# Chunk outputs and states of the second recurrence issued inside the next chunk's levels, with GpSimd held behind the block copies

## The chip, the cores and the metric

The kernel runs on one core of one Trainium2 chip. The metric is the device time of one execution in microseconds (us), the median of the runs. The engines are TensorE (PE, with its weight loads as PEld), VectorE (DVE), ScalarE (ACT), GpSimd (POOL) and SyncE (SP), which issues the loads. A time such as 1374.25 is us from the start of the profiled span.

## The reference, cut to what matters

The program is two transformer-like blocks over 512 tokens of width 1024. The first has two layers, and each layer has a mixer with two recurrences; the change is in the second one (HGRN2), which runs forward and backward over the sequence with four heads of 128:

```
def _hgrn2_scan(q, k, i, logf):
    # S_t = diag(f_t) S_{t-1} + k_t i_t^T,  o_t = S_t^T q_t
    def step(state, inp):
        q_n, k_n, i_n, b_n = inp          # b_n: running sum of logf in the chunk
        dec = jnp.exp(jnp.where(incl, b_n[:, :, :, None, :] - b_n[:, :, None, :, :], -jnp.inf))
        att = jnp.einsum('bhtd,bhsd,bhtsd->bhts', q_n, k_n, dec)
        o = (jnp.einsum('bhtd,bhdv->bhtv', q_n * jnp.exp(b_n), state)
             + jnp.einsum('bhts,bhsv->bhtv', att, i_n))
        last = b_n[:, :, -1:, :]
        state = (state * jnp.exp(last[:, :, 0, :])[..., None]
                 + jnp.einsum('bhsd,bhsv->bhdv', k_n * jnp.exp(last - b_n), i_n))
        return state, o
```

## The kernel before, in words

`hgrn_stage` does this once for each layer, so twice in an execution, with chunks of 128 tokens: four chunks `m` = 0 to 3. There are two lanes, `d` = 0 (forward) and 1 (backward), which go side by side. Every engine has its own instruction stream, written out by hand, and semaphores `S[...]` tie them; nothing reorders the streams.

The attention matrix `AT` of a chunk is built in seven levels, n = 0 to 6, of growing distance between query and key. For level n DVE makes scaled queries and keys (`scaled`, L1812 and L1813: two 128x256 products for a lane, both inputs in SBUF), and PE multiplies them (`level`, L1646 and L1649, `last_level`, L1660) into one of two accumulator banks of the lane. Levels 0 to 4 are merged by DVE into `AC` (`gather`, L1821), level 5 and level 6 are copied from PSUM into `AT` by ACT (`assembled`, L1763 and L1767), and the diagonal blocks `AC` are copied into `AT` by DVE (`blocks_placed`, L1832: four copies of 32x128 for a lane). The factors come from exponents: PE sums log decays (`exponents`, L1618 and L1619) into banks 0 to 3, and ACT exponentiates them (`decays`, L1753). `prepare` (L1596, L1604 and L1605) turns the next chunk's keys and sums, inside the levels of the chunk before it.

From `AT` PE makes the chunk's outputs (`outputs`, L139, with the part from the old state for m > 0) and its new state (`state`, L1679). Before, for chunks 0 and 1 these stand between one chunk's last level and the next chunk's first product (`diagonal`, L1629), and write the accumulator banks. Only chunk 2 has them inside the levels of chunk 3, in banks 0 to 3 (`late`). ACT copies the outputs out (L1800), DVE adds the new state to the decayed one (`grow_state`, L1854 for the first, L1852 afterwards), and ACT decays that for the next chunk (`state_decayed`, L1780).

GpSimd has four products of 128x512 at each of the chunk boundaries 0/1 and 1/2 and two at 2/3, both inputs in SBUF: `keys_decayed` (L1570) and `queries_decayed` (L1576). Before, the first of them waits for the last scaled product of the chunk, so it starts together with DVE's block copies.

Of the kernel before, what the change touches and what calls it, by code (L numbers as in the profile page):

```python
# [1506 lines left out]
def hgrn_stage(nc, signals, PS, C, CR, LF, KK, HI, HQ, X, O, new, early):  # L1507
# [21 lines left out]
    with signals.stage(*[f"hgrn_{n}{d}" for n in kinds for d in lanes]) as sems:  # L1529
# [5 lines left out]
        late = lambda m: m == CH - 2  # L1535
# [18 lines left out]
        with nc.Block() as block:  # L1554
# [8 lines left out]
            def _(pool):  # L1563
                def keys_decayed(m, d):
                    pool.wait_ge(S["es"][d], m + 1)
                    if m:
                        pool.wait_ge(S["x"][1], 2 * m * LEVELS)
                    if m == 2:
                        pool.wait_ge(S["st"][d], 1)
                    pool.tensor_tensor(kd_of(m, d), keys(m, d).rearrange("p (h n) -> p h n", h=4), B[d]["ES"][:, :, :], ALU.mult).then_inc(S["kd"][d], 1)  # L1570
# [20 lines left out]
            def _(pe):  # L1591
                def turned_keys(m, d):
                    if m:
                        pe.wait_ge(S["e"][1], 8 * m)
                    for h in H4:
                        last = pe.transpose(hx(d, h), keys(m, d)[:, h * P:(h + 1) * P], C[:, IDENT, :])  # L1596
                    last.then_inc(S["kt"][d], 1)

                def suffix(m, d):
                    pe.wait_ge(S["fl"][d], m + 1)  # L1600
                    if m:
                        pe.wait_ge(S["e"][1], 8 * m)
                    b = B[d]
                    pe.matmul(PS[:, 2 + d, :], CR[:, d, 8, :], b["FH"][:, :], start=True, stop=False)  # L1604
                    pe.matmul(PS[:, 2 + d, :], CR[:, d, 8, :], b["FL"][:, :], start=False, stop=True).then_inc(S["suf"][d], 1)  # L1605
# [15 lines left out]
                def diagonal(m, d):  # L1621
                    pe.wait_ge(S["ktc"][d], m + 1)
                    if m == CH - 1:
                        pe.wait_ge(S["af"][d], m)
                    elif m:
                        pe.wait_ge(S["oc"][d], m)
# [5 lines left out]
                def level(m, d, n):  # L1632
                    pe.wait_ge(S["x"][d], 2 * (m * LEVELS + n + 1))
                    if n >= 2:
                        pe.wait_ge(S["ac"][d], m * SMALL_LEVELS + n - 1)
                    elif n == 1:
                        pe.wait_ge(S["diac"][d], m + 1)
                    elif m == CH - 1:
                        pe.wait_ge(S["af"][d], m)
                    elif m:  # L1640
                        pe.wait_ge(S["su"][d], m)
# [50 lines left out]
                for m in range(CH):  # L1692
                    for d in lanes:
                        diagonal(m, d)
                    for n in range(LEVELS):
# [7 lines left out]
                        if m == CH - 1 and n in (1, 3):  # L1703
                            for e in lanes:
                                pe.wait_ge(S["e"][e], 8 * CH)
                            d = n // 2
                            outputs(CH - 2, d)
                            state(CH - 2, d)
# [9 lines left out]
                    for d in lanes:  # L1718
                        if not late(m):
                            outputs(m, d)  # L1720
                        if m < CH - 2:
                            state(m, d)

            @block.scalar
            def _(act):
# [29 lines left out]
                def assembled(m):  # L1755
                    for d in lanes:
                        act.wait_ge(S["a"][d], m * LEVELS + LEVELS - 1)
                        if m:
                            act.wait_ge(S["o"][d], m)
                        else:  # L1760
                            act.wait_ge(S["mk"][0], 5)
                        for one, two in zip(early_quarters[d], late_quarters[d]):
                            act.copy(B[d]["AT"][one, :, two], small(d, LEVELS - 2)[one])  # L1763
                    for d in lanes:
                        one, two = FIRST[d], SECOND[d]
                        act.wait_ge(S["a"][d], (m + 1) * LEVELS)
# [15 lines left out]

                for m in range(CH):
                    if 0 < m < CH - 1:
                        for d in lanes:
                            state_decayed(m, d)
                    decays(m, 1, 1)
                    if m + 1 < CH:
                        for d in lanes:
                            high(m + 1, d)  # L1790
                        prepared(m + 1)
# [5 lines left out]
                    if m < 2:  # L1797
                        for d in lanes:
                            act.wait_ge(S["o"][d], m + 1)
                            act.copy(of_chunk(chunk(m, d)), per_head(acc(d, 1))).then_inc(S["oc"][d], 1)  # L1800

            @block.vector
            def _(dve):
# [24 lines left out]
                def blocks_placed(m, d):  # L1828
                    dve.wait_ge(S["ac"][d], (m + 1) * SMALL_LEVELS)
                    dve.wait_ge(S["o"][d], m) if m else dve.wait_ge(S["mk"][0], 5)  # L1830
                    for rows in QUARTERS:
                        last = dve.tensor_copy(B[d]["AT"][rows, :, rows], B[d]["AC"][rows, :, :])  # L1832
# [28 lines left out]
                for m in range(CH):  # L1861
# [4 lines left out]
                    for n in range(LEVELS):  # L1866
                        if 0 < n < LEVELS - 1:
                            for d in lanes:
                                scaled(m, d, n + 1)
                        if n < SMALL_LEVELS:  # L1870
# [5 lines left out]
                        if m == CH - 1 and n in (2, 4):  # L1876
                            d = n // 2 - 1
                            add_output(CH - 2, d)
                            grow_state(CH - 2, d)
                    for d in lanes:  # L1880
                        blocks_placed(m, d)
                    if m + 1 < CH:
                        for n in range(2):
                            for d in lanes:
                                scaled(m + 1, d, n)
                    for d in lanes:
                        if m < CH - 2:
                            grow_state(m, d)
                        if m == CH - 1:
                            add_output(m, d)  # L1890
# [1527 lines left out]
```

## Time and profile before

| | us |
|---|---|
| runs, median of 3 | 2850.24 (2844.2 to 2854.49) |
| the profiled execution, its own time | 2841.33 |
| its span in the trace | 2839.5 |
| PE busy | 2726.6 (96% of the span) |
| DVE busy | 1513.2 (53%) |
| ACT busy | 1199.3 (42%) |
| POOL busy | 850.1 (30%) |

The two executions of the stage lie at 362.9 to 458.9 and at 1350.0 to 1443.3 of the span. The shares of the page are means over stages that have different limits; what the change is worth is decided in these two stretches, some 7% of the span.

### The profile page before, as it was taken

Reading aid. Unit: us, or ns where it says so; the run is one execution under the profiler, and the core shown is the slowest. Engines: PE = TensorE matmul, PEld = TensorE weight load, DVE = VectorE, ACT = ScalarE, POOL = GpSimd, SP = SyncE. Lnnn points to the kernel's source line nnn. Section 1 sums busy time; section 2 is a strip of 40 time slices with the busy share of each in tenths; the row PEclk is TensorE's granted clock in tenths of the full one; section 3 lists DMA queues with packets and bytes.
Section 4 is the critical chain, followed back from the end, with each engine's and each line's share of the span. In section 5 each row is a group of like instructions: output and inputs, shape, how many; then the busy total and the mean of one; then the engine's idle time right before and its main releaser. Section 6 shows DMA issues by size and latency. Waiting matters only on the chain. (4 is left out here: it accounts for less than half of the span.)

```text
span 2839.5 us, 48429 instructions
## 1 busy us (share of the span) xinstructions
PE 2726.6 (96%) x20434; PEld 2226.6 (78%) x20434; DVE 1513.2 (53%) x2273; ACT 1199.3 (42%) x1941; POOL 850.1 (30%) x476
## 2 busy tenths in 40 slices
PE   8989988999999999899989999999999999999999
PEld 6777877888888877778778888888787778888887
DVE  7565577357526475655863565364886543521120
ACT  5564665233212245645742332222545543442331
POOL 2343020024444423520200344443002224344433
PEclk9989999999999999899999999999999999999999
DMA  5102103333323331021033333232522223333322
GB/s 177 58 4 88 60 3 98 100 115 96 104 82 104 89 98 53 4 89 60 3 113 96 111 97 110 83 108 71 123 76 75 65 65 98 97 97 97 97 82 82
DMA packets 414585, 236.30 MB, mean 83 GB/s; under 512 B 24244, under 2 KB 404770, under 8 KB 413730
## 3 DMA queue, kind: packets, MB, share of 16 engines
q1 hardware_dynamic: 413490, 233.18, 28.2%
q8 instruction: 163, 2.67, 0.4%
q14 instruction: 52, 0.43, 0.1%
q10 hardware_dynamic: 880, 0.02, 0.0%
HBM read 226.88 MB, written 6.29 MB: 82 GB/s over the span
## 5 line engine op out<-in xcount | busy, mean ns | idle before, releaser
L2425 POOL TENSOR_TENSOR WLO<-RAW,WHI 128x1024 fp32r<-128x1024 f32 (+1 forms) x199 | 522.1, 2629 | 964.5 <-ACT WHI L2261 964.5
L146 PE MATMUL PS<-HHI,WHI 128*128 128x512 f32 x2016 | 795.8, 395 | 5.4 <-DVE WLO L3157 2.2
L147 PE MATMUL PS<-HLO,WHI 128*128 128x512 f32 x2016 | 787.2, 390 | 0.0
L148 PE MATMUL PS<-HHI,WLO 128*128 128x512 f32 x2016 | 786.7, 390 | 0.0
L146 PEld LDWEIGHTS PS<-HHI,WHI 128*128 128x128 f32 x2016 | 379.9, 188 | 98.1 <-issue 7.4
L147 PEld LDWEIGHTS PS<-HLO,WHI 128*128 128x128 f32 x2016 | 380.2, 189 | 80.3 <-issue 2.6
L148 PEld LDWEIGHTS PS<-HHI,WLO 128*128 128x128 f32 x2016 | 380.1, 189 | 79.8
L2261 ACT CAST WHI<-RAW 128x1024 fp32r<-128x1024 f32 (+1 forms) x202 | 221.7, 1102 | 508.4 <-PE PS L148 492.8
L2414 DVE TENSOR_TENSOR X<-X,PS 128x512 f32<-128x512 f32 x48 | 33.0, 688 | 334.1 <-PE PS L148 334.1
L3219 POOL TENSOR_TENSOR WLO<-RAW,WHI 128x1280 fp32r<-128x1280 f32 x31 | 91.3, 2947 | 317.7 <-ACT WHI L3102 317.7
L2397 DVE SCALAR_TENSOR_TENSOR ACC<-GP,PARS,ACC 128x512 f32<-128x512 f32 x88 | 163.0, 1853 | 3.1
L146 PE MATMUL PS<-MHI,WHI 128*128 128x512 f32 x384 | 150.4, 392 | 7.4 <-DVE LHID L2355 4.2
L148 PE MATMUL PS<-MHI,WLO 128*128 128x512 f32 x384 | 149.6, 390 | 0.0
L147 PE MATMUL PS<-MLO,WHI 128*128 128x512 f32 x384 | 149.5, 389 | 0.0
L202 ACT CAST WHI<-RAW 128x1536 fp32r<-128x1536 f32 (+1 forms) x50 | 81.6, 1632 | 99.1 <-PE PS L148 87.8
L2390 DVE TENSOR_TENSOR GP<-PS,RS 128x512 f32<-128x512 f32 x44 | 30.4, 692 | 152.5 <-PE PS L148 127.7
L206 DVE TENSOR_TENSOR WLO<-RAW,WHI 128x1536 fp32r<-128x1536 f32 (+1 forms) x50 | 97.3, 1946 | 22.8 <-ACT WHI L202 21.6
L2303 ACT ACTIVATE ACC<-ACC 128x512 f32<-128x512 f32 x44 | 27.9, 634 | 176.5 <-DVE ACC L2397 176.5
L146 PE MATMUL PS<-YHI,WHI 128*128 128x512 f32 x256 | 100.5, 393 | 1.5 <-DVE WLO L2359 1.2
L146 PE MATMUL PS<-WHI,HHI 128*128 128x512 f32 (+1 forms) x256 | 96.1, 375 | 5.1 <-DVE WLO L1456 5.1
L148 PE MATMUL PS<-YHI,WLO 128*128 128x512 f32 x256 | 99.7, 390 | 0.0
L147 PE MATMUL PS<-YLO,WHI 128*128 128x512 f32 x256 | 99.7, 389 | 0.0
(502 smaller groups left out, 4757.2 us busy)
## 6 DMA issues: line engine op xcount, KB each, us to landing
RAW<-in_w_up SPq DMA_DIRECT2D x88, 512.0 KB, 3.7
RAW<-in_w_mlp SPq DMA_DIRECT2D x64, 512.0 KB, 4.0
RAW<-in_w_in SPq DMA_DIRECT2D x46, 512.0 KB, 3.8
RAW<-in_w_down SPq DMA_DIRECT2D x32, 704.0 KB, 4.4
RAW<-in_w_in SPq DMA_DIRECT2D x20, 1024.0 KB, 5.0
RAW<-in_w_gate SPq DMA_DIRECT2D x32, 512.0 KB, 4.0
RAWQ<-in_w_in SPq DMA_DIRECT2D x24, 512.0 KB, 3.7
RAW<-in_w_out SPq DMA_DIRECT2D x24, 512.0 KB, 5.2
```

Source lines behind the costliest of these rows:

```text
L146: e.matmul(out, wh, xh, start=first and n == 0, stop=False)
L147: e.matmul(out, wh, xl, start=False, stop=False)
L148: last = e.matmul(out, wl, xh, start=False, stop=final and n == len(quads) - 1)
L202: self.hi_st.done(act.copy(self.hi[:, s], self.raw[:, s]), f"unit{s}")
L206: self.lo_st.done(dve.tensor_tensor(self.lo[:, s], self.raw[:, s], self.hi[:, s], ALU.subtract), f"unit{s}")
L2261: ac.done(act.copy(slot(WHI, u), source(u)), f"hi{u}")
L2303: ac.done(act.activation(acc, acc, ACT.Silu), f"silu{i}")
L2390: dv.done(dve.tensor_tensor(gp[:, 1:513], tile_bank((i, 0)), RS[:, :], ALU.mult), f"g{i}")
L2397: dv.done(dve.scalar_tensor_tensor(acc, gp[:, n:n + 512], tap(n), acc, ALU.mult, ALU.add), f"tap{n}_{i}")
L2414: dv.done(dve.tensor_tensor(X[:, m, :], X[:, m, :], PS[:, 6 + m % 2, :], ALU.add), f"x{g}_{m}")
L2425: pool.tensor_tensor(slot(WLO, u), source(u), slot(WHI, u), ALU.subtract).then_inc(lo_s, 1)
L3219: pool.tensor_tensor(WLO[:, u % 3], RAW[:, u % 3], WHI[:, u % 3], ALU.subtract).then_inc(lo_s, 1)
```

## The change

`late` now holds for chunks 0, 1 and 2. So the outputs and the state of chunk m-1 are issued in chunk m behind level 1 (lane 0) and level 2 (lane 1), and write banks 0 to 3, which the exponents use at other times. DVE's `grow_state` goes to the same levels (ahead of the gather of level 2 and of level 3), and ACT's copy of the outputs and `state_decayed` stand behind `decays(m, 1, 1)` and the casts of `high`. The copy of level 5 into `AT` (four 32x128 copies from PSUM for the two lanes of a chunk) goes from ACT to DVE (`level_placed`) behind the block copies, and the semaphore `as` is given only behind it. GpSimd's keys of chunk m wait for `as` of both lanes. The scaled products of levels 0 and 1 of the next chunk go lane by lane.

```
-        late = lambda m: m == CH - 2
+        late = lambda m: m < CH - 1
...
                 def keys_decayed(m, d):
                     pool.wait_ge(S["es"][d], m + 1)
                     if m:
-                        pool.wait_ge(S["x"][1], 2 * m * LEVELS)
+                        for e in lanes:
+                            pool.wait_ge(S["as"][e], m)
...
                 def turned_keys(m, d):
...
+                    if m > 1:
+                        pe.wait_ge(S["oc"][d], m - 1)
...
                 def suffix(m, d):
...
+                    if m > 1:
+                        pe.wait_ge(S["su"][d], m - 1)
...
                 def diagonal(m, d):
                     pe.wait_ge(S["ktc"][d], m + 1)
-                    if m == CH - 1:
-                        pe.wait_ge(S["af"][d], m)
-                    elif m:
-                        pe.wait_ge(S["oc"][d], m)
+                    if m:
+                        pe.wait_ge(S["as"][d], m)
...
-                        if m == CH - 1 and n in (1, 3):
+                        if m and n in (1, 2):
                             for e in lanes:
-                                pe.wait_ge(S["e"][e], 8 * CH)
-                            d = n // 2
-                            outputs(CH - 2, d)
-                            state(CH - 2, d)
+                                pe.wait_ge(S["e"][e], 8 * m + 8)
+                            outputs(m - 1, n - 1)
+                            state(m - 1, n - 1)
...
-                    for d in lanes:
-                        if not late(m):
-                            outputs(m, d)
-                        if m < CH - 2:
-                            state(m, d)
+                for d in lanes:
+                    outputs(CH - 1, d)
...
                 for m in range(CH):
-                    if 0 < m < CH - 1:
-                        for d in lanes:
-                            state_decayed(m, d)
                     decays(m, 1, 1)
                     if m + 1 < CH:
                         for d in lanes:
                             high(m + 1, d)
+                    if 0 < m < CH - 1:
+                        for d in lanes:
+                            output_kept(m - 1, d)
+                            state_decayed(m, d)
+                    if m + 1 < CH:
                         prepared(m + 1)
...
                     for rows in QUARTERS:
-                        last = dve.tensor_copy(B[d]["AT"][rows, :, rows], B[d]["AC"][rows, :, :])
+                        dve.tensor_copy(B[d]["AT"][rows, :, rows], B[d]["AC"][rows, :, :])
+
+                def level_placed(m, d):
+                    dve.wait_ge(S["a"][d], m * LEVELS + LEVELS - 1)
+                    for one, two in zip(early_quarters[d], late_quarters[d]):
+                        last = dve.tensor_copy(B[d]["AT"][one, :, two], small(d, LEVELS - 2)[one])
                     last.then_inc(S["as"][d], 1)
...
+                        if m and n in (2, 3):
+                            grow_state(m - 1, n - 2)
...
-                        if m == CH - 1 and n in (2, 4):
-                            d = n // 2 - 1
-                            add_output(CH - 2, d)
-                            grow_state(CH - 2, d)
+                        if m == CH - 1 and n in (2, 3):
+                            add_output(CH - 2, n - 2)
                     for d in lanes:
                         blocks_placed(m, d)
+                    for d in lanes:
+                        level_placed(m, d)
                     if m + 1 < CH:
-                        for n in range(2):
-                            for d in lanes:
+                        for d in lanes:
+                            for n in range(2):
                                 scaled(m + 1, d, n)
-                    for d in lanes:
-                        if m < CH - 2:
-                            grow_state(m, d)
```

Two places show how the streams move. The first is DVE at the boundary of chunks 0 and 1, in the first layer. Before (L1832 are the block copies, L1812 and L1813 the scaled products, L1854 `grow_state`, L1865 the masked diagonal):

```order
L1832 COPY hAT_1<-hAC_1 32x4x32 x8
L1812 TENSOR_TENSOR hX_1<-HQ,X 128x256
L1813 TENSOR_TENSOR hX_1<-hKT_1,X 128x256
L1812 TENSOR_TENSOR hX_1<-HQ,hE_1 128x256
L1813 TENSOR_TENSOR hX_1<-hKT_1,hE_1 128x256
L1812 TENSOR_TENSOR hX_1<-HQ,X 128x128x2
L1813 TENSOR_TENSOR hX_1<-hKT_1,X 128x128x2
L1812 TENSOR_TENSOR hX_1<-HQ,hE_1 128x128x2
L1813 TENSOR_TENSOR hX_1<-hKT_1,hE_1 128x128x2
L1854 COPY hST_1<-PS 128x512 x2
L1865 TENSOR_TENSOR hAC_1<-PS,hEYE 128x128 x2
```

And in the changed kernel, where lines have other numbers:

```order
L1824 COPY hAT_1<-hAC_1 32x4x32 x8
L1829 COPY hAT_1<-PS 32x4x32 x4
L1804 TENSOR_TENSOR hX_1<-HQ,X 128x256
L1805 TENSOR_TENSOR hX_1<-hKT_1,X 128x256
L1804 TENSOR_TENSOR hX_1<-HQ,X 128x128x2
L1805 TENSOR_TENSOR hX_1<-hKT_1,X 128x128x2
L1804 TENSOR_TENSOR hX_1<-HQ,hE_1 128x256
L1805 TENSOR_TENSOR hX_1<-hKT_1,hE_1 128x256
L1804 TENSOR_TENSOR hX_1<-HQ,hE_1 128x128x2
L1805 TENSOR_TENSOR hX_1<-hKT_1,hE_1 128x128x2
L1862 TENSOR_TENSOR hAC_1<-PS,hEYE 128x128 x2
```

Four PSUM copies have come in (L1829), lane 1's products stand behind both of lane 0's, and `grow_state` has left for the levels of chunk 1.

The second is PE behind the last exponents of the same boundary. Before (L139 the outputs, L1679 the states, L1629 the diagonal, L1646 levels):

```order
L139 MATMUL PS<-hAT_1,HI 128x128 x4
L1679 MATMUL PS<-HI,RAW 128x128 x4
L139 MATMUL PS<-hAT_1,HI 128x128 x4
L1679 MATMUL PS<-HI,RAW 128x128 x4
L1629 MATMUL PS<-HQ,hKT_1 32x32 x32
L1646 MATMUL PS<-hX_1 32x32 x32
```

In the changed kernel the boundary has `L1632 MATMUL PS<-HQ,hKT_1 32x32 x32` and level 0 at once, then the exponents of lane 1, and then:

```order
L1647 MATMUL PS<-hX_1 32x32 x32
L139 MATMUL PS<-hAT_1,HI 128x128 x4
L1680 MATMUL PS<-HI,RAW 128x128 x4
L1647 MATMUL PS<-hX_1 32x32 x32
L139 MATMUL PS<-hAT_1,HI 128x128 x4
L1680 MATMUL PS<-HI,RAW 128x128 x4
L1647 MATMUL PS<-hX_1 32x32 x32
```

The outputs and the state of each lane of chunk 0 now stand behind levels 1 and 2 of chunk 1. The number of matmuls is the same.

## Rows read from the trace of the kernel before

**Rows 1.** Windows; columns: span, busy of PE, PEld, DVE, ACT, POOL; PEclk; DMA; GB/s

```profile
362.90:458.90 96.00, 85.47 (x2064) 71.41 (x2064) 79.84 (x222) 60.30 (x133) 17.82 (x14) 0.95 0.07 19
1350.00:1443.30 93.30, 83.51 (x2073) 68.97 (x2071) 79.75 (x222) 60.59 (x134) 17.83 (x14) 1.00 0.08 20
393.70:418.40 24.70, 22.49 (x527) 18.82 (x526) 20.88 (x53) 16.86 (x40) 5.03 (x4) 0.93 0.01 4
1383.00:1405.10 22.10, 21.13 (x525) 17.86 (x524) 20.84 (x53) 16.49 (x39) 5.09 (x4) 1.00 0.01 4
```

**Rows 2.** Timeline of PE, second layer: start, duration, engine, line, operation, [idle before <- releaser]

```profile
1379.37 1.05 PE L139 MATMUL PS<-hAT,HI 128*128 128x128 f32 x8
1383.04 0.76 PE L1629 MATMUL PS<-HQ,hKT 128*32 128x32 f32 x64
...
1388.70 1.01 PE L1646 MATMUL PS<-hX 128*32 128x32 f32 x64 [0.60 <-DVE hX L1813]
...
1399.71 0.38 PE L139 MATMUL PS<-hQE,hST 128*128 128x128 f32 x2
...
1404.17 1.06 PE L1679 MATMUL PS<-HI,KK 128*128 128x128 f32 x8
...
1437.65 0.69 PE L1660 MATMUL PS<-hX 128*64 128x64 f32 x16 [2.69 <-DVE hX L1813]
1438.80 0.46 PE L139 MATMUL PS<-hQE,hST 128*128 128x128 f32 x2 [0.47 <-issue]
```

**Rows 3.** Timeline of DVE, second layer

```profile
1374.25 5.88 DVE L1832 COPY hAT<-hAC 32x128 f32<-32x128 f32 x8
1382.85 1.29 DVE L1854 COPY hST<-PS 128x512 f32<-128x512 f32 x2
1387.27 0.60 DVE L1821 COPY_PREDICATED hAC<-hMASK,PS 128x128 f32<-128x128 int32 x2 [0.57 <-PE PS L1646]
1405.27 0.69 DVE L1852 TENSOR_TENSOR hST<-hSD,PS 128x512 f32<-128x512 f32 x1 [0.49 <-PE PS L1679]
1409.07 0.60 DVE L1821 COPY_PREDICATED hAC<-hMASK,PS 128x128 f32<-128x128 int32 x2 [0.81 <-PE PS L1646]
1437.30 1.85 DVE L1832 COPY hAT<-hAC 32x128 f32<-32x128 f32 x8
```

**Rows 4.** Timeline of POOL, second layer

```profile
1374.50 2.59 POOL L1570 TENSOR_TENSOR KK<-KK,RAW 128x512 f32<-128x512 f32 x2 [15.07 <-DVE hX L1813]
1377.06 1.28 POOL L1576 TENSOR_TENSOR hQE<-HQ,X 128x512 f32<-128x512 f32 x1
```

**Rows 5.** Timelines of POOL and DVE, first layer, boundary of chunks 2 and 3

```profile
433.26 1.34 POOL L1576 TENSOR_TENSOR hQE<-HQ,hE 128x512 f32<-128x512 f32 x1 [1.30 <-ACT hE L1753]
433.48 1.41 DVE L1812 TENSOR_TENSOR hX<-HQ,X 128x256 f32<-128x256 f32 x1
```

**Rows 6.** Timelines of POOL and DVE in the feed-forward stage, same contention

```profile
609.97 2.40 POOL L2425 TENSOR_TENSOR WLO<-RAW,WHI 128x1024 fp32r<-128x1024 f32 x1 [175.37 <-ACT WHI L2261]
613.03 8.04 POOL L2425 TENSOR_TENSOR WLO<-RAW,WHI 128x1024 fp32r<-128x1024 f32 x3 [0.67 <-ACT WHI L2261]
...
613.62 2.38 DVE L2329 SCALAR_TENSOR_TENSOR HLO<-X,PARS,HHI 128x512 fp32r<-128x512 f32 x1 [2.96 <-ACT HHI L2285]
```

**Rows 7.** One line, L1170 of DVE (32x128 with a PSUM input): ns min/median/max

```profile
L1170 DVE TENSOR_TENSOR AT<-PS,DM x8: 277/286/296, 133.5 to 155.2; 32x128 f32<-32x128 f32 x8
```

**Rows 8.** Timeline of ACT: level 5's copies into `AT`

```profile
1377.52 1.05 ACT L1763 COPY hAT<-PS 32x128 f32<-32x128 f32 x4
```

**Rows 9.** PE idle and granted clock, first layer: timeline, then windows

```profile
401.12 0.64 PE L1646 MATMUL PS<-hX 128*32 128x32 f32 x48 [1.73 <-issue]
450.81 1.12 PE L1660 MATMUL PS<-hX 128*64 128x64 f32 x16 [2.69 <-DVE hX L1813]
...
402.20:405.60 3.40, 3.40 (x65) 2.56 (x67) 2.17 (x9) 2.37 (x4) 0.00 (x0) 0.50 0.02 5
450.00:456.80 6.80, 5.53 (x37) 5.40 (x37) 2.81 (x11) 0.73 (x2) 0.00 (x0) 0.50 0.88 233
```

More of the change, by code:

```diff
@@ L1637, in level @@
                         pe.wait_ge(S["diac"][d], m + 1)
-                    elif m == CH - 1:
+                    elif m:
                         pe.wait_ge(S["af"][d], m)
-                    elif m:
-                        pe.wait_ge(S["su"][d], m)
                     x = B[d][f"X{n % 2}"]
@@ L1756, in assembled @@
                     for d in lanes:
[L1757 to L1763, printed above, removed]
-                    for d in lanes:
                         one, two = FIRST[d], SECOND[d]
+                        act.wait_ge(S["o"][d], m) if m else act.wait_ge(S["mk"][0], 5)
                         act.wait_ge(S["a"][d], (m + 1) * LEVELS)
@@ L1781, in state_decayed, with output_kept @@
                     last.then_inc(S["sd"][d], 1)
+                def output_kept(m, d):
+                    act.wait_ge(S["o"][d], m + 1)
+                    act.copy(of_chunk(chunk(m, d)), per_head(out_bank(m, d))).then_inc(S["oc"][d], 1)
                 for m in range(CH):
-                    if 0 < m < CH - 1:
-                        for d in lanes:
-                            state_decayed(m, d)
                     decays(m, 1, 1)
@@ L1796, in _ @@
                         decays(m + 1, 0, 1)
-                    if m < 2:
-                        for d in lanes:
-                            act.wait_ge(S["o"][d], m + 1)
-                            act.copy(of_chunk(chunk(m, d)), per_head(acc(d, 1))).then_inc(S["oc"][d], 1)
             @block.vector
@@ L1875, in _ @@
                                 low(m + 1, d)
-                        if m == CH - 1 and n in (2, 4):
-                            d = n // 2 - 1
-                            add_output(CH - 2, d)
-                            grow_state(CH - 2, d)
+                        if m == CH - 1 and n in (2, 3):
+                            add_output(CH - 2, n - 2)
                     for d in lanes:
                         blocks_placed(m, d)
+                    for d in lanes:
+                        level_placed(m, d)
                     if m + 1 < CH:
-                        for n in range(2):
-                            for d in lanes:
+                        for d in lanes:
+                            for n in range(2):
                                 scaled(m + 1, d, n)
-                    for d in lanes:
-                        if m < CH - 2:
-                            grow_state(m, d)
-                        if m == CH - 1:
-                            add_output(m, d)
+                for d in lanes:
+                    add_output(CH - 1, d)
 FIRST_OUT = 4
```

## The prediction

> **What bounds the kernel now.** I read the page first: PE is busy for 96% of the span (the table above), so over the whole kernel PE is the bound. The windows of the stage that is changed say more. In the two layers it takes 96.0 and 93.3 us, with PE busy 85.5 and 83.5 and DVE 79.8 in each [rows 1]. Chunk 1 of the second layer has 21.1 us of PE and 20.8 us of DVE in 22.1 [rows 1]: two engines stand at 95%, each in strict order, and there is little idle time for anybody to win back. The PE timeline shows where PE does wait: 0.60 us inside the levels of chunk 1 and 2.69 us ahead of the very last level, both for DVE's scaled products [rows 2]. The DVE timeline shows where DVE waits: 0.57, 0.49 and 0.81 us for PE [rows 3]. And it shows one DVE row that is far too long: the eight block copies take 5.88 us at the boundary 0/1, while POOL runs its four products [rows 3, 4], and 1.85 us at the end, where POOL is silent [rows 3]. That is what the change is after, together with the stretch of 1379.37 to 1383.04, and of 1399.71 to about 1405.2, in which PE makes outputs and states between two chunks [rows 2].
>
> An upper bound on any gain comes first. All of PE's work stays, so only PE's idle time can go. In the second layer that is about 1 us in the middle chunks. In the first layer it is about 2.6 us more: its chunk 1 takes 24.7 us against 22.1 [rows 1], since PE idles 1.73 us and then runs 3.4 us at half the granted clock [rows 9]. With the ends untouched that is some 5 us, under 0.2% of the kernel.
>
> **Part 1, PE's outputs and states move into the levels.** At the boundary 0/1 this takes 1383.04 - 1379.37 = 3.7 us out, and the same 3.7 us come back behind levels 1 and 2; at 1/2 it is about 5.4 us. The matmuls are the same, so the sum on PE is 0. The gain is only what PE fills of its own gaps, and that needs DVE to be on time for the next chunk's level 0.
>
> **Part 2, DVE's stream.** From 1380.13 (1374.25 + 5.88) to 1382.85 stand eight scaled products [rows 3]: 0.34 us each.
> - Level 5's copies come from ACT, where four took 1.05 us [rows 8] and were hidden: ACT's busy time is 16.5 of 22.1 us [rows 1], so taking them away gives nothing. On DVE the nearest row is a 32x128 operation on PSUM, 0.29 us [rows 7]; the block copies from SBUF are 1.85 / 8 = 0.23 us. So four cost 0.9 to 1.2 us; I take 1.2, because L1170 also reads PSUM. Over chunks 0 to 2 that is +3.6 us on DVE.
> - The block copies at the boundaries 0/1 and 1/2 no longer meet POOL: 5.88 - 1.85 = 4.0 us each go.
> - But POOL now starts when the copies end, which is when the scaled products start. Each of them reads two SBUF tiles, and there is one such row under a POOL product: 1.41 us instead of 0.42, ending at 434.89, 0.29 us behind POOL's end at 434.60 [rows 5]. POOL too is drawn out: three products take 8.04 us where one alone takes 2.40 [rows 6], so a 512-wide DVE operation between two of them adds some 0.4 us, and a 256-wide one by my estimate 0.2. Only one DVE operation gets in for each POOL product. Four POOL products at 1.28 [rows 4] are 5.1 us, with three such additions and the 0.29 us of the last DVE product 6.0 us, in which DVE has done four products that cost 1.36 us alone. The loss is 4.6 us, where the copies lost 4.0. So the lock is not taken away but moved: +0.6 us for each of two boundaries, +1.2 us. Bounds: nothing lost at all (the row would be an accident), or 5.5 us if POOL is drawn out by the full 0.4.
> - `grow_state` (1.29 us for two, rows 3) only moves.
>
> The Trainium skill, SBUF — State Buffer, section Who interferes with whom, says that a DVE instruction with two SBUF inputs contends with a GpSimd instruction that reads SBUF, and that one with at most one SBUF input outside the two-port modes does not. That speaks against this change: by it all eight products are exposed and the level copies are not. The single L1812 row agrees; if it did not hold, this part would come out 9 us lower in each layer's DVE stream, which is rival 1.
>
> **Part 3, waits that go and come.** PE reaches the exponents of lane 1 a little earlier, and DVE's waits of 0.57, 0.49 and 0.81 us vanish: -1.9 us. In turn `grow_state` stands ahead of the gather of level 2 and waits for outputs and state. For chunk 0 PE needs 1.8 us behind level 1, while DVE has a gather and four products to do (0.4 + 1.34 = 1.7): +0.1. For chunk 1 PE needs 2.7 us ((1405.2 - 1399.71) / 2): +0.9. The sum of both is +1.0 us. On ACT `state_decayed` of lane 1 now waits for a `grow_state` that stands behind four more products, and the next chunk's keys and exponents are behind it; this makes PE about 2 us late for the last levels, which is hidden as long as DVE has its copies to do then.
>
> **Part 4, the end of the stage.** The outputs of chunk 3 started 1438.80 - 1437.30 = 1.5 us behind the start of the block copies [rows 2, 3]. Now `as` of lane 0 comes after all eight (1.85) and two level copies (0.6), at 2.45: +0.95 us, in the open.
>
> **The sum.** For one layer 3.6 + 1.2 - 1.9 + 1.0 + 0.95 = +4.85 us, for both +9.7. Off that goes what the first layer can win: its extra 2.6 us of idle time and low clock in chunk 1 [rows 1, 9], since 1.8 us of outputs now stand just ahead of where PE idled. But new idle time takes its place. At the boundary PE is done with exponents, diagonal and lane 0 at about 1380.5, and lane 1's products are ready only at 1374.25 + 1.85 + 1.2 + 6.0 + 0.7 = 1384.0: 3.5 us idle, where there was work. So I count half, -1.3 us. The sum is +8.4 us, and with parts of the waits hidden I take +7.5. The profiled execution is 2841.33, so it would be 2849 in its terms; against the median of the runs, 2850.24, it is 2857.5.
>
> **Rivals.**
> 1. The scaled products are not held by POOL; rows 5 are an accident. For it: it is one row. Against: it ends just behind POOL, and rows 6 have the same on other lines (2.38 us). Then DVE has its products at about 1380, PE goes on without a gap, and PE is the bound: about -1 us in the second layer, -3.6 in the first, +0.95 twice at the ends, about -3 to -4: 2846.5.
> 2. The new idle time costs clock. In the first layer 1.73 us and 2.69 us of idle PE are followed by half the granted clock, 1.2 instead of 2.4 GHz, for 3.4 and 6.8 us [rows 9]; in the second layer the same 2.69 us leave PEclk at 1.00 over the stage [rows 1, 2]. There are six new gaps of 2 to 3.5 us (three boundaries in two layers). Behind each stand eight exponent matmuls that would take 3.4 us instead of 1.8, and outputs twice as long, of which DVE's slack hides some 0.6: about 2 us each, +12 in all if every one falls, 2866 to 2870. It decides from about the third fall on, where the total passes +0.3%. This is the case on the other side: slower. The Trainium skill, TensorE: Matmul & The Clock Gate, section What's actually happening, says that full clock is only held by recent activity; by it every such gap puts the clock at risk. The trace agrees in two of these three gaps.
> 3. The change does less than it says: POOL's queries of chunk 3 don't wait for `as`, so the copies at the boundary 2/3 are held as before, and if ACT and PE hide the rest the sum is +0 to +2: 2851.
>
> **How the numbers follow.** What a measurement of this kernel can tell from no change is about 0.3%, 8.6 us. The forecast (+1 to +14 by the bounds of the copies, 0.9 to 1.2, of the lock and of the half that I counted) has 0.70: 0.42 of it below +8.6, 0.28 above. Rival 1 has 0.10 (0.07 same, 0.03 faster, by the spread of runs), rival 2 0.15 (0.14 slower, 0.01 same), rival 3 0.05 (same). That gives faster 0.03, same 0.55, slower 0.42. The range from 2846 to 2869 leaves out the better half of rival 1 and the upper end of rival 2.
>
> **What would show it.** The eight block copies at 1.85 us at the boundaries 0/1 and 1/2, and 4 us at 2/3; four of the eight scaled products behind them over 1 us each; L1829 near 0.29 us; POOL's four products in some 5.7 us; an idle PE of about 3.5 us ahead of level 0 of lane 1; a stage of about 97 to 98 us in the second layer. Scaled products at 0.42 us would make me wrong in the part on the lock; a granted clock of 0.5 in more than two stretches of the stage would be rival 2; a stage shorter than 93 us in the second layer would mean that I have missed a wait that PE had.

## The result and the profile after

The changed kernel takes 2870.1 us (median of four runs, 2868.2 to 2875.2) against 2849.4 for the kernel before: a ratio of 1.0073 (95% interval 1.0057 to 1.0088), 20.7 us slower. The forecast was 2857.5, in a range of 2846 to 2869; rival 2 (new idle time of TensorE costs clock) stood at 2866 to 2870 and had 0.15.

The windows of the changed kernel, with the columns of [rows 1]: both stages, then the boundaries 0/1 and 1/2 and the end of the stage in the second layer.

```profile
364.40:469.90 105.50, 90.00 (x2064) 73.55 (x2064) 84.34 (x238) 57.24 (x117) 18.75 (x14) 0.90 0.07 18
1368.15:1473.40 105.25, 88.56 (x2064) 72.87 (x2064) 84.40 (x238) 56.69 (x117) 18.74 (x14) 0.92 0.07 18
1396.00:1405.00 9.00, 5.91 (x202) 4.57 (x202) 7.57 (x17) 3.59 (x8) 3.33 (x3) 0.81 0.01 2
1420.00:1432.00 12.00, 9.08 (x218) 7.27 (x217) 9.17 (x21) 4.72 (x9) 3.39 (x3) 0.72 0.01 3
1460.00:1473.40 13.40, 8.32 (x123) 7.69 (x111) 8.04 (x27) 0.73 (x2) 0.00 (x0) 0.75 0.47 120
```

The stage grew from 96.0 and 90.5 us to 105.5 and 105.3, with the same 2064 matmuls. (The second window of [rows 1] begins 2.8 us ahead of the stage; from 1352.80 on it is 90.5 us long, with PE busy for 81.7.) PE is busy for 90.0 and 88.6 us where it was 85.5 and 81.7: that is no new work, it is work at a lower granted clock, 0.90 and 0.92 over the stages against 0.95 and 1.00. DVE has 4.5 us more.

DVE at the boundary 0/1 of the second layer, then the end of the stage (columns as in [rows 3]):

```profile
1390.55 1.83 DVE L1824 COPY hAT<-hAC 32x128 f32<-32x128 f32 x8
1392.40 1.21 DVE L1829 COPY hAT<-PS 32x128 f32<-32x128 f32 x4
1394.30 1.06 DVE L1804 TENSOR_TENSOR hX<-HQ,X 128x256 f32<-128x256 f32 x1 [0.69 <-PE PS L1661]
1395.28 1.51 DVE L1805 TENSOR_TENSOR hX<-hKT,X 128x256 f32<-128x256 f32 x1
1396.72 1.49 DVE L1804 TENSOR_TENSOR hX<-HQ,X 128x256 f32<-128x256 f32 x1
1398.13 1.48 DVE L1805 TENSOR_TENSOR hX<-hKT,X 128x256 f32<-128x256 f32 x1
1399.53 0.41 DVE L1804 TENSOR_TENSOR hX<-HQ,hE 128x256 f32<-128x256 f32 x1
...
1429.42 0.73 DVE L1813 COPY_PREDICATED hAC<-hMASK,PS 128x128 f32<-128x128 int32 x2 [2.16 <-PE PS L1647]
1433.12 0.69 DVE L1849 TENSOR_TENSOR hST<-hSD,PS 128x512 f32<-128x512 f32 x1 [1.64 <-PE PS L1680]
...
1441.86 2.92 DVE L1824 COPY hAT<-hAC 32x128 f32<-32x128 f32 x8
...
1463.78 1.83 DVE L1824 COPY hAT<-hAC 32x128 f32<-32x128 f32 x8
1465.62 1.21 DVE L1829 COPY hAT<-PS 32x128 f32<-32x128 f32 x4
```

POOL at the boundary 0/1:

```profile
1393.78 2.73 POOL L1571 TENSOR_TENSOR KK<-KK,RAW 128x512 f32<-128x512 f32 x2 [19.00 <-DVE hAT L1829]
1396.46 1.47 POOL L1577 TENSOR_TENSOR hQE<-HQ,X 128x512 f32<-128x512 f32 x1
1397.89 1.44 POOL L1577 TENSOR_TENSOR hQE<-HQ,hE 128x512 f32<-128x512 f32 x1
```

The block copies take 1.83 us instead of 5.88, and the hold has moved to the scaled products behind them: four take 1.06 to 1.51 us, one for each product of POOL, and the fifth, behind POOL's end, 0.41.

PE at the boundaries 0/1 and 1/2 and at the end (columns as in [rows 2]):

```profile
1396.84 0.46 PE L1647 MATMUL PS<-hX 128*32 128x32 f32 x32
1400.33 0.66 PE L1647 MATMUL PS<-hX 128*32 128x32 f32 x32 [3.03 <-DVE hX L1805]
1400.92 0.80 PE L1623 MATMUL PS<-CR,hFH 128*128 128x512 f32 x1
...
1424.40 0.66 PE L1647 MATMUL PS<-hX 128*32 128x32 f32 x32 [2.92 <-DVE hX L1805]
1426.01 0.63 PE L1623 MATMUL PS<-CR,hFH 128*128 128x512 f32 x1
...
1461.51 0.45 PE L1650 MATMUL PS<-hX 128*32 128x32 f32 x16 [1.13 <-DVE hX L1805]
1464.12 0.69 PE L1661 MATMUL PS<-hX 128*64 128x64 f32 x16 [1.49 <-DVE hX L1805]
1466.26 0.79 PE L139 MATMUL PS<-hQE,hST 128*128 128x128 f32 x2 [1.46 <-DVE hAT L1829]
```

Lane 1's level 0 waits 3.03 and 2.92 us for its scaled products, and the exponents behind it take 0.63 us each where those ahead of the gap took 0.39, and start 0.43 us apart instead of 0.23. In the first layer the same two gaps are 2.89 and 2.97 us, again with half the clock behind or around them. By the clock's record the two stages hold 20.5 and 17.1 us at 0.50, against 10.2 and 0 before [rows 9]. Behind the level copies DVE itself first waits 0.69 us, for PE's last level (1394.30).

### The profile page after: what moved, and what is told of

Its sections match the earlier page's. It is cut to its first block and busy times, and to the rows that moved or that the text cites. A ratio compares the mean times of both kernels' runs of the same rounds, so it can differ in the third digit from the quotient of the medians.

```text
span 2873.4 us, 48449 instructions
## 1 busy us (share of the span) xinstructions
PE 2737.2 (95%) x20434; PEld 2230.5 (78%) x20434; DVE 1522.1 (53%) x2305; ACT 1193.1 (42%) x1909; POOL 852.1 (30%) x476
## 5 line engine op out<-in xcount | busy, mean ns | idle before, releaser
L206 DVE TENSOR_TENSOR WLO<-RAW,WHI 128x1536 fp32r<-128x1536 f32 (+1 forms) x50 | 97.3, 1946 | 23.0 <-ACT WHI L202 21.8
```

The source lines that it names most:

```text
L206: self.lo_st.done(dve.tensor_tensor(self.lo[:, s], self.raw[:, s], self.hi[:, s], ALU.subtract), f"unit{s}")
```

## The experiments

Sixteen kernels, each timed in five rounds beside the kernel before on its own chip. Theory T1: the hold moves onto the scaled products, DVE has its copies besides, PE idles at the boundaries and runs at the lower clock behind that. Rival T2: outputs and states inside the levels cost by themselves. "+" is the difference of medians against the kernel before of the same set; chunks are measured from one DVE `diac` product to the next (the last one to the end of the stage).

| kernel | us | ratio (95% interval) |
|---|---|---|
| changed kernel | +20.7 | 1.0073 (1.0057 to 1.0088) |
| a_pool_early | +13.9 | 1.0051 (1.0037 to 1.0066) |
| b_filler | +16.0 | 1.0056 (1.0044 to 1.0068) |
| c_level_act | +14.4 | 1.0052 (1.0038 to 1.0067) |
| d_dve_products | +8.4 | 1.0031 (1.0019 to 1.0042) |
| n_after_filler | +4.8 | 1.0027 (1.0012 to 1.0041) |
| g_act_and_dve | +6.1 | 1.0026 (1.0013 to 1.0038) |
| h_outputs_only | +5.4 | 1.0020 (1.0008 to 1.0032) |
| e_before_pool_late | -1.4 | 0.9999 (0.9988 to 1.0010) |
| f_before_dve_products | +7.6 | 1.0031 (1.0019 to 1.0043) |
| i_chunk3_before | +5.6 | 1.0019 (1.0009 to 1.0030) |
| j_grow_behind | +9.3 | 1.0033 (1.0020 to 1.0046) |
| k_both | +5.6 | 1.0022 (1.0013 to 1.0031) |
| l_both_dve | +7.3 | 1.0027 (1.0015 to 1.0039) |
| p_moved_filler | +0.6 | 1.0005 (0.9996 to 1.0013) |
| m_before_filler | -2.1 | 0.9995 (0.9986 to 1.0003) |
| o_late_filler | -1.7 | 0.9998 (0.9989 to 1.0006) |

### One part undone at a time

**a_pool_early**, the changed kernel with POOL's keys waiting as before:

```
-                        for e in lanes:
-                            pool.wait_ge(S["as"][e], m)
+                        pool.wait_ge(S["x"][1], 2 * m * LEVELS)
```

> The changed kernel with one part undone: GpSimd's keys wait for the last scaled product again, not for the block copies. Theory 1 (the lock between POOL and DVE is only moved from the copies to the scaled products, and PE idles about 3 us at the boundary either way, after which its clock falls): the copies are back at 5.9 us, the scaled products at 0.42 us, lane 1's first product is ready within 1 us of where it is in the changed kernel, and the time stays at +15 to +22 us against the kernel before. Theory 2 (putting GpSimd behind the copies is what costs, since scaled products are what PE waits for): most of the 21 us goes, to +3 to +8 us.

2862.3 us. Its DVE has the held copies back, and no scaled product is held; its PE has two short gaps in place of the long one. Timelines of DVE and PE in this kernel, boundary 0/1:

```profile
1381.70 5.88 DVE L1823 COPY hAT<-hAC 32x128 f32<-32x128 f32 x8
...
1388.83 0.43 DVE L1803 TENSOR_TENSOR hX<-HQ,X 128x256 f32<-128x256 f32 x1
```

```profile
1388.32 0.46 PE L1631 MATMUL PS<-HQ,hKT 128*32 128x32 f32 x32 [1.12 <-DVE hAT L1828]
...
1390.99 0.46 PE L1646 MATMUL PS<-hX 128*32 128x32 f32 x32 [0.88 <-DVE hX L1804]
1391.38 0.50 PE L1622 MATMUL PS<-CR,hFH 128*128 128x512 f32 x1
```

The exponents behind them run at 0.50 and 0.39 us. DVE loses the same 4 us either way; only the place of PE's wait differs, and with it the clock: its two stages hold 20.5 us at 0.50 in all, against 37.6. That is worth 6 us (by the ratios) to 7 (by the differences). +13.9 lies below the range of the first theory and above that of the second; the first had PE idle as long as before, and it idles 2.0 us at this boundary instead of 3.0.

**c_level_act**, level 5's copies back on ACT, the diagonal waiting for `af`:

```
-                    for d in lanes:
-                        level_placed(m, d)
...
+                        for one, two in zip(early_quarters[d], late_quarters[d]):
+                            act.copy(B[d]["AT"][one, :, two], small(d, LEVELS - 2)[one])
```

> The changed kernel with level 5's copies back on ACT. DVE loses four copies of 0.30 us in each chunk. Theory 1 (DVE's chain is the bound of the stage at each boundary and at the end): -1.2 us for three chunks and -0.6 at the end, -4.2 us for a layer, -8 in all, so +12 to +14 us against the kernel before; the PE gap at the boundary shrinks from 3.0 to 1.8 us, which may save one or two falls of the clock more. Theory 2 (the copies are hidden behind PE): 0 to -2 us.

2862.7 us, just above the first theory's +12 to +14. The gaps at the boundaries shrink to 1.83 to 1.96 us, and two of the four (1.92 and 1.95) still have half the clock behind them, for 3.4 us. But DVE does not get to its products any earlier. At the boundary 0/1 of the second layer:

```profile
1384.48 1.85 DVE L1828 COPY hAT<-hAC 32x128 f32<-32x128 f32 x8
1388.28 1.04 DVE L1808 TENSOR_TENSOR hX<-HQ,X 128x256 f32<-128x256 f32 x1 [1.95 <-PE PS L1661]
...
1392.09 0.41 DVE L1809 TENSOR_TENSOR hX<-hKT,X 128x256 f32<-128x256 f32 x1
```

The first product starts 3.80 us behind the start of the block copies, and 3.75 in the changed kernel: PE's last level sets it in both. The level copies fill a wait of DVE there. What they cost is that GpSimd, which waits for them, starts later, so that four products are held here instead of three.

**d_dve_products**, POOL's products of chunks 1 to 3 made by DVE inside the chunk, behind the gathers of levels 1 and 2:

```
+                        if 0 < m < CH - 1 and n == 1:
+                            for d in lanes:
+                                keys_decayed(m, d)
+                        if m and n == 2:
+                            for d in lanes:
+                                queries_decayed(m, d)
```

> The changed kernel with the products that POOL made (keys of chunks 1 and 2, queries of 1 to 3) made by DVE, behind the gathers of level 1 and 2, where DVE waits for PE. Nothing of POOL then runs beside DVE in chunks 1 to 3. DVE gets four products of 0.6 us, 2.4 us for a chunk, and loses the lock's 4.6. Theory 1 (the lock at the boundary causes gap and clock): the scaled products take 0.42 us, the PE gap ahead of lane 1's level 0 is under 1 us, the clock stays at 1.00 there, and the time falls to -2 to +6 us against the kernel before. Theory 2 (outputs and states inside the levels are what costs, through grow_state's waits): it stays at +12 us or more.

2856.8 us, between its two ranges: with nothing held at the boundaries and more work on DVE, the stages are 95.9 and 96.1 us and chunk 0 falls from 22.2 to 17.3 in the second layer. Without POOL's hold more than half of the loss is gone.

**h_outputs_only**, both undone: POOL as in a, level 5's copies as in c. Only outputs, states and the order of the scaled products are changed.

> The changed kernel without the GpSimd part and without the level copies on DVE: only outputs and states are moved, and the order of the scaled products. If the parts add up (GpSimd part 7.9 us, level copies 7.4 us off 2870.1): 2855 us, +6 against before. T1 (with the gaps at the boundaries goes the clock): under 2853 us, stages under 96 us, half clock only where the kernel before has it. T2 (the move itself costs): 2856 to 2861 us, chunks 2 and 3 of the second layer 3 to 5 us longer than before.

2851.2 us, +5.4, between the theories. The windows of chunks 0 to 3 in the second layer, first the kernel before:

```profile
1363.36:1384.04 20.68, 19.09 (x494) 15.74 (x480) 20.12 (x53) 14.50 (x32) 5.08 (x4) 1.00 0.01 4
1384.04:1405.86 21.82, 20.85 (x514) 17.57 (x505) 20.39 (x53) 16.78 (x41) 5.09 (x4) 1.00 0.01 3
1405.86:1424.04 18.18, 17.42 (x550) 13.57 (x544) 17.19 (x52) 14.41 (x33) 2.61 (x2) 1.00 0.02 4
1424.04:1443.34 19.30, 15.17 (x390) 13.73 (x388) 14.77 (x47) 3.83 (x10) 0.00 (x0) 1.00 0.33 85
```

and h_outputs_only:

```profile
1367.66:1387.60 19.94, 16.29 (x501) 12.58 (x489) 19.08 (x51) 12.96 (x28) 5.08 (x4) 1.00 0.02 4
1387.60:1408.97 21.37, 19.71 (x509) 15.75 (x509) 20.46 (x53) 16.32 (x38) 5.06 (x4) 1.00 0.01 3
1408.97:1430.90 21.93, 21.33 (x525) 17.70 (x526) 18.74 (x53) 16.46 (x38) 2.71 (x2) 1.00 0.01 3
1430.90:1453.70 22.80, 17.91 (x392) 15.91 (x392) 14.98 (x47) 4.03 (x11) 0.00 (x0) 0.93 0.28 72
```

Chunk 0 gives 2.8 us of PE away and is only 0.7 shorter, since DVE is its bound (19.08 of 19.94). Chunk 2 gets 3.9 us of PE and is 3.8 longer: there PE is the bound (21.33 of 21.93). "The sum on PE is 0" is right, but the work went from a chunk with slack in PE into one without. Chunk 3 is 3.5 longer, part of it at a lower clock (0.93).

In the first layer the two stages are equally long (95.4 us from PE's first matmul to its last). There h's chunk 1 is 3.2 us shorter (21.4 against 24.6), and that is the chunk in which the kernel before has 3.4 us at half clock [rows 9]. Each profile is one execution, so the 5.4 us are to be taken from the medians.

**g_act_and_dve**, c and d together, tells the same from the other side.

> The changed kernel without both causes of a late level 0: level 5's copies back on ACT, and GpSimd's products of chunks 1 to 3 on DVE. Outputs and states stay inside the levels. T1 (lock, level copies and the clock are the whole loss): the stage is at 93 to 95 us in both layers, 2846 to 2851 us. T2 (outputs and states inside the levels cost by themselves, as DVE waits 1.4 to 2.2 us for PE behind levels 1 and 2 and chunks 2 and 3 grow): 2852 to 2858 us, with chunks 2 and 3 near 22 and 24 us.

2852.0 us, T2's value, with chunks 2 and 3 at 22.3 and 24.2 us in the second layer.

### The kernel before with one part alone

**e_before_pool_late**: the inverse of a's edit, put into the kernel before.

> The kernel before with one part of the change: GpSimd's scaled keys wait for the block copies of both lanes. T1 (the lock is only moved, and costs where PE has nothing else to do): here PE still has outputs and states between the chunks, so the held products find PE at work. Copies 1.85 us, four scaled products near 1.5 us, state ahead of the next chunk some 2 us later for want of its keys: 0 to +3 us a layer, 2848 to 2855 us, no new stretch at half clock. T3 (the GpSimd part costs some 7 us by itself, as undoing it in the changed kernel gave back 7.9 us): 2855 to 2857 us.

2844.4 us, no difference. Its DVE has nearly the hold of the changed kernel, three products of 1.49 to 1.54 us where that has four; DVE, then PE:

```profile
1374.62 1.85 DVE L1833 COPY hAT<-hAC 32x128 f32<-32x128 f32 x8
1377.93 1.54 DVE L1813 TENSOR_TENSOR hX<-HQ,X 128x256 f32<-128x256 f32 x1 [1.45 <-PE PS L1661]
1379.39 1.50 DVE L1814 TENSOR_TENSOR hX<-hKT,X 128x256 f32<-128x256 f32 x1
1380.81 1.49 DVE L1813 TENSOR_TENSOR hX<-HQ,hE 128x256 f32<-128x256 f32 x1
```

```profile
1379.68 1.05 PE L139 MATMUL PS<-hAT,HI 128*128 128x128 f32 x8
...
1382.36 1.06 PE L1680 MATMUL PS<-HI,RAW 128*128 128x128 f32 x8
1383.34 0.76 PE L1630 MATMUL PS<-HQ,hKT 128*32 128x32 f32 x64
1384.73 1.06 PE L1647 MATMUL PS<-hX 128*32 128x32 f32 x64 [0.63 <-DVE hST L1855]
```

PE fills the time of the hold (1377.9 to 1382.3) with exponents, outputs and states. So the GpSimd part costs its 6 to 7 us only once the outputs are gone from there: T1's mechanism, and T3 (it costs by itself) falls. Of the 4.0 us that the copies give back, DVE spends 1.45 waiting for PE's last level, and the held products take the rest.

**f_before_dve_products**: d's edit, put into the kernel before.

> The kernel before with GpSimd's scaled keys and queries of chunks 1 to 3 made by DVE behind the gathers of levels 1 and 2, where DVE waits for PE; nothing of GpSimd then meets the block copies. T1: each boundary loses 4 us of held copies and gains up to 4 x 0.55 = 2.2 us of DVE work inside the chunk: -1 to -2 us per boundary, three boundaries in two layers, less what PE is the bound for; 2840 to 2846 us. T2 (DVE's stream is the bound in the middle of a chunk and every operation there comes out at PE): 2846 to 2852 us.

2853.5 us, above both ranges: my expectation was wrong. Chunk 0 of the second layer, which has no hold now and no added product, takes 20.3 us instead of 20.7, so the held copies had cost that chunk 0.4 us and not 4. Without the hold the two `grow_state` copies wait for PE instead. Later the added products delay the levels (the two key products are the last row), and chunk 1 grows from 21.8 to 24.2 us. DVE:

```profile
1386.55 0.69 DVE L1862 COPY hST<-PS 128x512 f32<-128x512 f32 x1 [0.96 <-PE PS L1673]
1388.33 0.69 DVE L1862 COPY hST<-PS 128x512 f32<-128x512 f32 x1 [1.09 <-PE PS L1673]
1392.64 1.29 DVE L1804 TENSOR_TENSOR KK<-KK,RAW 128x512 f32<-128x512 f32 x2
```

### The clock by itself

**b_filler** and **n_after_filler** leave the changed kernel as it is and put useless 128x512 matmuls, whose result nobody reads, into PE's idle times. b: 12 ahead of lane 1's level 0 in chunks 1 to 3.

```
+                    if m and d == 1 and n == 0:
+                        pe.wait_ge(S["af"][1], m)
+                        for k in range(12):
+                            pe.matmul(acc(1, 0), CR[:, 1, 8, :], B[1]["FH"][:, :], start=True, stop=True)
```

> The changed kernel with 12 matmuls of 128x512 that do nothing useful, issued by PE in the gap ahead of lane 1's level 0 of chunks 1 to 3 (about 2.7 us at full clock, a gap of 3 us before). Theory 1 (idle PE costs the clock, and that is most of what the forecast missed): PEclk is 1.00 behind the boundaries, the exponents behind them take 1.8 instead of 3.4 us, and the time falls by 6 to 12 us, to +9 to +15 us against the kernel before. Theory 2 (the clock is a side effect, DVE's longer chain is what costs): the time stays at +18 to +24 us or rises by what the fillers take beyond the gap.

2864.3 us, 1 us above the first theory's range. Half clock at the boundaries is gone; chunks 1 and 2 of the second layer fall from 24.1 and 24.7 to 22.9 and 22.1 us, but at the boundary 2/3 there had been a gap of 0.5 us only, and chunk 3 is 2 us longer for fillers that stand in the way. n puts 10 at the boundaries 0/1 and 1/2, none at 2/3, and 4, 6 and 5 into the three waits at the end of the stage:

```
+                    if m == CH - 1 and n == LEVELS - 2 and d == 0:
+                        useless(4)
...
+                    if m == CH - 1:
+                        useless(6)
...
+                useless(5)
```

> The changed kernel with useless 128x512 matmuls in its idle times: 10 ahead of lane 1's level 0 in chunks 1 and 2, 4 ahead of level 5, 6 ahead of the last level and 5 ahead of the outputs in chunk 3, none at the boundary 2/3 where b_filler put them in the way. T1: no half clock in either stage but at its start; b_filler's -5.8 us, 4 us more for what its 12 at the boundary 2/3 cost, and 3 to 5 us for the end: 2855 to 2861 us. Rival (what b_filler gave is all that the clock costs, the rest is waiting for DVE): 2861 to 2865 us.

2852.4 us: 70 matmuls more, and the kernel is 16 us faster by the differences, 0.46% by the ratios (1.0073 and 1.0027), some 13 us. It fell below T1's range. The half clock in the two stages fell from 37.6 to 3.4 us. PE at the boundary 1/2 of its first layer, then its stages:

```profile
417.83 2.25 PE L1644 MATMUL PS<-hFH,CR 128*128 128x512 f32 x9
420.57 0.46 PE L1658 MATMUL PS<-hX 128*32 128x32 f32 x32 [0.49 <-DVE hX L1819]
420.96 0.50 PE L1623 MATMUL PS<-CR,hFH 128*128 128x512 f32 x1
```

```profile
364.40:464.50 100.10, 92.68 (x2099) 74.56 (x2099) 84.55 (x238) 56.51 (x117) 18.83 (x14) 0.98 0.07 19
1357.20:1455.70 98.50, 91.76 (x2099) 73.85 (x2099) 84.98 (x238) 56.17 (x117) 18.97 (x14) 1.00 0.08 19
```

**m_before_filler** puts 9 such matmuls ahead of the last level of chunk 3 in the kernel before, **o_late_filler** in e_before_pool_late, **p_moved_filler** in i_chunk3_before (below).

> The kernel before with 9 useless 128x512 matmuls (0.23 us each, 2.1 us) ahead of the last level of chunk 3, where PE waits 2.69 us for DVE. T1 (idle TensorE costs clock): the half clock at the end of the stage goes; in the first layer of the profile it made the outputs of chunk 3 0.42 us apart instead of 0.22 for 6.8 us, some 2.6 us; up to -2.5 us per layer, 2841 to 2845 us. Rival (the half clock behind 2.69 us comes anyway or costs nothing that counts): 2846 to 2849 us.

> e_before_pool_late (0.9999 of the time before) with the same 9 useless matmuls as m_before_filler. If the two have nothing to do with each other, the same time as m_before_filler to 1.5 us.

> i_chunk3_before (outputs and states moved, chunk 3 as before; 1.0019) with the same 9 useless matmuls ahead of the last level. Its loss against m_before_filler is what the move costs without the clock at the end: if the move costs plain work's order (PE's outputs taken from chunk 0, where DVE is the bound, into chunk 2, where PE is), +3 to +5 us against m_before_filler, 2846 to 2850 us; if it was the clock, 0 to +2.

m 2845.5, o 2846.0, p 2848.2 us. In m the gap of 2.69 us is 0.43, and no half clock is left at the stage's end in either layer, but the gain, 0.05%, cannot be told from nothing. On p it is at the edge of the noise: 1.0019 (1.0009 to 1.0030) becomes 1.0005 (0.9996 to 1.0013). p is 2.7 us behind m, which has the same fillers, between the two ranges of its expectation, and 1.0005 against 0.9995 is not certain either. The outputs may then stand in either place at nearly the same time; p is no faster than before. n is 6.9 us behind m (1.0027 against 0.9995): that is what is left of the changed kernel's loss when both have fillers in their long gaps.

### Where in the levels

**i_chunk3_before** is h with chunk 3 as it was (outputs of chunk 2 behind levels 1 and 3, `grow_state` behind the gathers of levels 2 and 4), **j_grow_behind** is h with `grow_state` behind the gather instead of ahead of it, **k_both** both, **l_both_dve** the same on g.

```
+                        if m == CH - 1 and n in (2, 4):
+                            add_output(CH - 2, n // 2 - 1)
+                            grow_state(CH - 2, n // 2 - 1)
```

> h_outputs_only (outputs and states moved, nothing else; 1.0020 of the time before) with chunk 3 as it was: outputs and states of chunk 2 behind levels 1 and 3, grow_state behind the gathers of levels 2 and 4. T2 (the move costs by the two grow_state that DVE has to wait for ahead of a gather, 1.35 and 0.65 us in chunk 3): chunk 3 from 22.7 to 20.5 to 21 us in both layers, -4 us, 2847 us, 1.0005 to 1.001. T1 (chunk 3 is longer for the clock or its end): less than 1.5 us off, 2849 to 2851 us.

> h_outputs_only with grow_state behind the gathers of levels 2 and 3 instead of ahead of them, in all chunks. T2: DVE still waits for PE there, but the gather, and with it level 3, no longer stands behind that wait; 0.7 to 1.3 us for each of the three chunks 1, 2 and 3 in two layers, -4 to -7 us: 2844 to 2847 us. Rival: PE is behind DVE at these places (it must do outputs and state before the next level anyway), and the gather cannot start earlier than level 2 is done: -0 to -2 us, 2849 to 2851 us.

> Both: chunk 3 as before, and grow_state behind the gathers in chunks 1 and 2. If T2 holds in full, 2843 to 2846 us, faster than before by up to 0.1%. If only chunk 3 matters, 2847 us as i_chunk3_before.

> The same as k_both, but with GpSimd's products of chunks 1 to 3 on DVE as in g_act_and_dve (1.0026), so that no copy and no product is held. If the shorter chunk 0 of that kernel (17 us against 20) and the better chunk 3 add up: stages of 92 to 94 us, 2842 to 2847 us. If DVE's stream is the bound of the chunks (its four more products of 0.55 us each come out in full): 2847 to 2850 us, no better than k_both.

i 2852.9, j 2856.6, k 2852.8, l 2854.5 us, all four above every range that I had given. Chunk 3 became 1.0 us shorter in i (21.7), which the medians don't show, and j made nothing better: `grow_state` ahead of the gather was not the cost, and that form of T2 falls. None of them beats the kernel before.

## Why the prediction was wrong

**The step that failed** is the term for the clock: "So I count half, -1.3 us". The new idle time was priced only as a smaller gain, and its cost was put into rival 2 with 0.15. Rival 2 is what happened. Of some 20 us, about 13 are the clock and the waits that it brings (n_after_filler). It shows in PE's busy time too: 90.0 and 88.6 us where h_outputs_only does the same matmuls in 84.5 and 84.3, some 5 us per layer. A stretch at half clock held up DVE as well: the wait of 2.16 us at 1429.42 is for a level behind eight exponents at 0.43 us. That rival 2's number (2866 to 2870) came so near is partly luck. It counted six new gaps of some 2 us each; there were four long ones, the two at 2/3 had about 0.5 us and full clock, and 6.8 us at half clock stood instead at the end of each stage, behind three waits of 1.1 to 1.5 us.

The other steps, as the prediction put them:
- **Level copies, 1.2 us a boundary**: measured 1.21, but not as time added to DVE's stream at 0/1 and 1/2. They fill its wait for PE's last level and start GpSimd later (c_level_act), which made the gap 1.1 us longer (3.03 against 1.95).
- **Lock moved, +0.6 us a boundary**: four scaled products took 5.23 us (1394.30 to 1399.53) where they cost 1.36, so 3.9 us were lost, not 4.6, and the copies had lost 4.0: about 0. POOL took 5.55 us against 5.7. Rival 1 did not come. The Trainium skill, SBUF — State Buffer, section Who interferes with whom, says that a DVE instruction with two SBUF inputs contends with a GpSimd instruction that reads SBUF. The trace agrees: 1.06 to 1.51 us under POOL, 0.41 behind it.
- **PE idle 3.5 us at the boundary**: 3.03 and 2.92.
- **Boundary 2/3, 4 us**: 2.92, with one scaled product of 1.29 us behind it; the gap in PE there is 0.56, not one of the "six new gaps".
- **DVE's waits of 0.57 and 0.81 us vanish**: they grew to 1.40 and 2.16 us (the same two gathers, in chunks 1 and 2). In h_outputs_only, which has no long gap at the boundaries, they are 0.22 each. So this term of -1.9 us fell with the step above.
- **grow_state, +0.1 and +0.9**: 0.43 in chunk 1 (for chunk 0), 1.64 + 0.19 in chunk 2. Chunk 3, which the prediction left out, has 1.45 + 0.69; with its old order (i_chunk3_before) it is 1.0 us shorter.
- **End of the stage, +0.95 us**: the outputs start 1466.26 - 1463.78 = 2.48 us behind the copies against 1.5, +0.98; not foreseen were 6.8 us at half clock behind the three waits.
- **PE's sum is 0**: right over the stage, wrong by chunk. The move alone costs 0.20% (0.08 to 0.32), and chunk 2 shows how. With chunk 3 in its old order and fillers at the end of the stage, it is 0.10% (p against m), which the noise covers.
- **The held copies as the thing to win**: an error in how the rows were read. 5.88 us for 1.85 us of work is a loss only if somebody waits; PE had outputs and states to do meanwhile. e and f, which take the hold off the copies, gain nothing, and f's chunk 0 shows 0.4 us.
- **Two sums**: rival 1's terms (-1, -3.6 and twice +0.95) add up to -2.7 us, not to -3 to -4, and 2850.24 + 7.5 is 2857.7. Neither bears on the result.

The clock may also sit behind the sizes of parts a and c; that is argued, not shown. They differ from the changed kernel by 0.22 and 0.21%, h, which has both, by 0.53%, so they don't add up simply; with these intervals the difference of 0.10% is not certain.

**Left open**: no run takes back the lane-by-lane order of the scaled products alone. It puts lane 1's level 0 behind two more products, by the rows of the boundary 0/1 some 0.7 us of the gap of 3.03 (1399.53 to 1400.20). Open too is why c's gaps of 1.83 and 1.96 us kept their clock and those of 1.92 and 1.95 did not, and how the remaining 0.27% of n_after_filler divides between chunk 2's load on PE, the level copies and the fillers themselves, which cannot be told at this resolution.

## What to carry to other kernels

Before moving work of the bounding engine out of a place, ask what it was covering there: here the outputs filled the time in which DVE was held, and hid it. Balance two engines chunk by chunk, not over the stage. A new wait of TensorE has two prices, its own length and, often, the clock behind it; some useless matmuls in the gap measure the second, without undoing anything.

## What was not expected of the hardware

- 70 additional matmuls of 128x512 in idle time made a kernel of 2870 us some 13 to 16 us faster, the granted clock in its stages 0.98 and 1.00 instead of 0.90 and 0.92. The Trainium skill, TensorE: Matmul & The Clock Gate, section What's actually happening, says that activity releases the throttle; these runs agree.
- All four boundary gaps of 2.89 to 3.03 us stood with half clock, but in the second layer a gap of 2.69 us in the kernel before, one of 2.25 in o_late_filler and one of 1.69 in m_before_filler left it whole. So the length of a gap alone does not decide it. Every stretch at half clock in the stages lasted 3.4 or 6.8 us.
- At the boundaries 0/1 and 1/2 one DVE product of 128x256 gets in for each POOL product of 128x512, and POOL's queries take 1.44 to 1.47 us there, against 1.28 to 1.31 in the kernel before.
